# Seven half products for eight: one Strassen step in the down and output projections of a streaming encoder

## What is computed

```python
def swiglu(x, w_gate, w_up, w_down):
    return (jax.nn.silu(x @ w_gate) * (x @ w_up)) @ w_down        # 1024 -> 2816 -> 1024

for l in range(2):
    x = x + 0.5 * swiglu(rmsnorm(x, ffn1_norm[l]), ...)
    h = rmsnorm(x, mix_norm[l])
    x = x + (conv_mixer(h) if l == 0 else attn_mixer(h))          # ends in @ w_out / @ w_o, 1024 -> 1024
    x = x + 0.5 * swiglu(rmsnorm(x, ffn2_norm[l]), ...)
y = rmsnorm(x, final_norm)
```

## Time and profile before

| | |
|---|---|
| median of 3 runs | 2298.11 us (2297.57 to 2299.38) |
| span of the profiled execution, first to last instruction | 2295.8 us |
| busy: TensorE, VectorE, ScalarE, GpSimd | 99%, 43%, 28%, 4% |
| matmuls | 16584 |

### The profile page before, as it was taken

How to read it: one execution, slowest core, us unless ns; L and a number is a source line. 1 busy time by engine, 2 the same in 40 slices (tenths; PEclk the granted TensorE clock), 3 DMA queues, 4 the chain that set the end, 5 groups by cost and what they waited for, 6 DMA issues and landing times.

```text
span 2295.8 us, 39703 instructions
## 1 busy us (share of the span) xinstructions
PE 2267.1 (99%) x16584; PEld 2201.1 (96%) x16584; DVE 978.2 (43%) x1309; ACT 646.0 (28%) x967; POOL 101.6 (4%) x109
## 2 busy tenths in 40 slices
PE   7999999999999999999999999999999999999997
PEld 7999999999999999999999999987878899999997
DVE  5433333555443333345333433455455444333334
ACT  4212212422332122124221212334343432122122
POOL 1000000200100000002000000100000110000002
PEclk9999999999999999999999999999999999999999
DMA  4222222222222222223222222222222122222222
GB/s 148 83 83 83 83 83 74 86 89 83 83 77 87 80 82 82 82 72 93 83 83 83 83 83 81 85 75 73 73 72 74 57 83 80 85 78 87 76 81 69
DMA packets 55407, 187.91 MB, mean 82 GB/s; under 512 B 6864, under 2 KB 7168, under 8 KB 55312
## 3 DMA queue, kind: packets, MB, share of 16 engines
q1 hardware_dynamic: 49248, 173.76, 25.2%
q10 hardware_dynamic: 3888, 7.70, 0.9%
q0 software_dynamic: 2176, 5.09, 0.9%
HBM read 179.42 MB, written 7.09 MB: 81 GB/s over the span
## 4 chain that ended last, share of the span: by engine, by line
PE 98%; DVE 1%; DMA 1%; ACT 0%; ACTq 0%; DVEq 0%; issue 0%
PE ps L829 92%; PE ps L909 2%; PE ps L891 2%; PE ps L877 1%; DMA x<-x_t 1%; PE ps L912 0%; PE ps L844 0%; DVE sumsq L664 0%; DVE x L810 0%; PE ps L894 0%; PE ps L896 0%; DVE rstd L611 0%; PE ps L866 0%; PE ps L914 0%; ACTq L460 0%; DVE w_lo L601 0%
## 5 line engine op out<-in xcount | busy, mean ns | idle before, releaser
L829 PE MATMUL ps<-xg_hi,w_hi 128*128 128x288 f32 x3584 | 780.0, 299 | 11.1 <-DVE w_lo L601 8.6
L829 PE MATMUL ps<-xg_hi,w_lo 128*128 128x288 f32 x3584 | 768.2, 296 | 0.0
L829 PE MATMUL ps<-xg_lo,w_hi 128*128 128x288 f32 x3584 | 767.2, 296 | 0.0
L829 PEld LDWEIGHTS ps<-xg_hi,w_hi 128*128 128x128 f32 x3584 | 576.0, 189 | 42.7 <-issue 26.5
L829 PEld LDWEIGHTS ps<-xg_lo,w_hi 128*128 128x128 f32 x3584 | 577.8, 189 | 0.0
L829 PEld LDWEIGHTS ps<-xg_hi,w_lo 128*128 128x128 f32 x3584 | 577.6, 189 | 0.0
L399 ACT ACTIVATE w_hi<-w_raw 128x1024 fp32r<-128x1024 f32 (+1 forms) x336 | 346.0, 1030 | 433.6 <-PE ps L829 398.9
L601 DVE TENSOR_TENSOR w_lo<-w_raw,w_hi 128x1024 fp32r<-128x1024 f32 (+1 forms) x336 | 402.5, 1198 | 27.2 <-ACT w_hi L399 27.1
L675 DVE TENSOR_TENSOR scaled<-ps,rstd 128x576 f32<-128x576 f32 x176 | 133.3, 758 | 640.6 <-PE ps L829 640.4
L829 PE MATMUL ps<-hid_hi,w_hi 128*128 128x288 f32 x1664 | 358.2, 297 | 1.7 <-DVE hid_lo L646 1.7
L829 PE MATMUL ps<-hid_hi,w_lo 128*128 128x288 f32 x1664 | 357.2, 296 | 0.0
(11 more groups left out here) (85 smaller groups left out, 852.3 us busy)
## 6 DMA issues: line engine op xcount, KB each, us to landing
w_raw<-w SPq DMA_DIRECT2D x304, 512.0 KB, 3.6
w_raw<-w SPq DMA_DIRECT2D x32, 384.0 KB, 3.0
x<-x_t ACTq DMA_DIRECT2D x8, 288.0 KB, 10.4
k_t<-k_sb ACTq DMA_DIRECT2D x8, 288.0 KB, 2.1
v_t<-v_sb ACTq DMA_DIRECT2D x8, 288.0 KB, 2.4
bias<-bias_ext POOLq DMA_DIRECT2D x16, 128.0 KB, 3.1
bias<-bias_ext POOLq DMA_DIRECT2D x16, 112.0 KB, 2.7
y_t<-x SPq DMA_DIRECT2D x6, 288.0 KB, 2.3
```

Of the source, the lines that this page charges most:

```text
L829: mm = pe.matmul(ps[:, 2 * out_slot + b, 0:HALF], wt[:, w_slot, w], xt[:, k, b * HALF:(b + 1) * HALF], start=(k == 0 and n == 0), stop=(k ...
```

## The change

The down projections and `conv_out` are done in quads: two output tiles together, m and m+4. The weights of a quad are four blocks A11, A12, A21, A22, each half of the depth by 128 outputs, and the hidden operand is four blocks (two halves of the hidden tiles, two halves of the tokens). Seven products of sums of blocks, in Winograd's form of Strassen's step, give the four output blocks that eight products gave. Each half product is 3 x k/2 matmuls of 288 columns.

Sums of hidden blocks are made in the up phase for each pair of hidden tiles (`pair_sums`: four operations of 288 columns; `pair_hi` and `pair_lo` split the seven results in three parts: early, direct and late). Sums of weight blocks are made on VectorE, in place in a tile called the chain, between the splits: `first_sums`, then one add after the split of group 1 and one after group 2. The seven weights of a quad are split in four groups (g1 to g3 of two, g4 of one). Partial results are taken out of PSUM by ScalarE as snapshots, since a bank goes on accumulating, and VectorE makes four passes over `x` for a quad (two over snapshots, two over PSUM), where it made two.

Around this: the loops are unrolled, chunks are 8, 6 and 8 hidden tiles, `x` tiles are handled in the order 0, 4, 1, 5, ..., weight slots are three rings of two half-depth places and one place for g4, the weight blocks of a quad come in four loads of 256 KB (192 KB at depth 6), and several buffers of the attention share the memory of the new tiles, so that its first bias and cache loads start with the `qkv` phase.

```diff
-FFN_CHUNKS = (8, 8, 6)
+FFN_CHUNKS = (8, 6, 8)
...
+                if p.quads:
+                    for it in p.items:
+                        if it.u + 1 < QUADS:
+                            for b in range(3):
+                                load_direct(p.items[it.u + 1], b)
+                        if it.u + 2 < QUADS:
+                            load_chain(p.items[it.u + 2])
...
+            def load_direct(it, block_of):
+                width = it.phase.kh * P
+                if it.quad >= 1:
+                    if block_of == RAW_A22:
+                        sp.wait_ge(w_split, QUAD_ITEMS[it.quad - 1].steps["g3"].count)
+                    else:
+                        sp.wait_ge(chain_step, SUMS * (it.quad - 1) + block_of + 3)
...
+            def quads(p):
+                for it in p.items:
+                    g1, g2, g3, g4 = it.ahead
...
+                    act.wait_ge(tile_done, it.done + P1)
+                    if before:
+                        act.wait_ge(tile_read, before.evicted + 1)
+                    act.activation(snap[:, 0, :], ps[:, bank_a, 0:HALF], ACT.Copy).then_inc(snapped, 1)
+                    act.wait_ge(tile_done, it.done + P5)
+                    if before:
+                        act.wait_ge(tile_read, before.evicted + 2)
+                    act.activation(snap[:, 3, :], ps[:, bank_b, 0:HALF], ACT.Copy).then_inc(snapped, 1)
+                    split_hi(g1)
+                    act.wait_ge(tile_done, it.done + P6)
+                    act.activation(snap[:, 1, :], ps[:, bank_a, 0:HALF], ACT.Copy).then_inc(snapped, 1)
+                    split_hi(g2)
+                    split_hi(g3)
+                    if p.feeds is not None:
+                        act.wait_ge(tile_read, it.evicted + 1)
+                        if p.feeds < N_NORM - 1:
+                            xg_upper(p.feeds, first)
+                    act.wait_ge(tile_done, it.done + P7)
+                    act.activation(snap[:, 2, :], ps[:, bank_a, 0:HALF], ACT.Copy).then_inc(snapped, 1)
+                    if p.feeds is not None:
+                        squares(p.feeds, first)
+                        act.wait_ge(tile_read, it.evicted + 2)
+                        if p.feeds < N_NORM - 1:
+                            xg_upper(p.feeds, second)
+                        elif it.u == 0:
+                            act.preload_act_table(ACT.Sqrt)
+                        squares(p.feeds, second)
+                    split_hi(g4)
...
+                if w.part == "g1":
+                    first_sums(it)
+                dve.wait_ge(w_hi_done, w.count)
...
+                dve.tensor_tensor(group(w_lo, w), raw_group(w), group(w_hi, w).bitcast(F32),
+                                  ALU.subtract).then_inc(w_split, 1)
+                if w.part in ("g1", "g2"):
...
+                    dve.tensor_tensor(w_quad[:, chain, 0:width], w_quad[:, chain, 0:width], w_quad[:, direct, 0:width],
+                                      ALU.add).then_inc(chain_step, 1)
...
+                dve.tensor_tensor(w_quad[:, s3, 0:width], w_quad[:, chain, 0:width], w_quad[:, RAW_A11, 0:width],
+                                  ALU.add).then_inc(chain_step, 1)
+                dve.wait_ge(chain_step, SUMS * it.quad + 1)
+                dve.tensor_tensor(w_quad[:, chain, 0:width], w_quad[:, chain, 0:width], w_quad[:, RAW_A22, 0:width],
+                                  ALU.add).then_inc(chain_step, 1)
...
+                    split_lo(g1)
+                    split_lo(g2)
+                    dve.wait_ge(snapped, shots + 3)
+                    dve.scalar_tensor_tensor(halves(x[:, m, :]), snap[:, 0:2, :], share, halves(x[:, m, :]),
+                                             ALU.mult, ALU.add).then_inc(x_part, 1)
+                    dve.wait_ge(tile_done, it.done + P3)
+                    dve.wait_ge(x_part, 2 * it.quad + 1)
+                    dve.scalar_tensor_tensor(halves(x[:, m, :]), banks(it.slot), share, halves(x[:, m, :]),
+                                             ALU.mult, ALU.add).then_inc(tile_read, 1)
+                    split_lo(g3)
+                    dve.wait_ge(snapped, shots + 4)
+                    dve.scalar_tensor_tensor(halves(x[:, m2, :]), banks(it.slot + 1), -share, halves(x[:, m2, :]),
+                                             ALU.mult, ALU.add).then_inc(x_part, 1)
                     if p.feeds is not None and p.feeds < N_NORM - 1:
...
+                        norm_lo(p.feeds, 2 * it.u)
+                    dve.wait_ge(x_part, 2 * it.quad + 2)
+                    dve.scalar_tensor_tensor(halves(x[:, m2, :]), snap[:, 2:4, :], -share, halves(x[:, m2, :]),
+                                             ALU.mult, ALU.add).then_inc(tile_read, 1)
+                    if p.feeds is not None and p.feeds < N_NORM - 1:
+                        norm_lo(p.feeds, 2 * it.u + 1)
+                    split_lo(g4)
...
+                    pe.wait_ge(w_split, it.steps["g1"].count)
+                    half_product(it, a, s1, B11, 1, True)
+                    half_product(it, b, s1 + 1, T1, 1, True)
+                    pe.wait_ge(w_split, it.steps["g2"].count)
+                    half_product(it, c, s2, B21, 2, True)
+                    pe.wait_ge(snapped, shots + 1)
+                    half_product(it, a, s2 + 1, T2, 3, False)
+                    pe.wait_ge(w_split, it.steps["g3"].count)
+                    half_product(it, d, s3, T4, 3, True)
+                    pe.wait_ge(snapped, shots + 2)
+                    half_product(it, b, s3 + 1, B22, 2, False)
+                    pe.wait_ge(w_split, it.steps["g4"].count)
+                    pe.wait_ge(snapped, shots + 3)
+                    half_product(it, a, 6, T3, 3, False)
```

More of the change, by code:

```diff
@@ new lines, in plan @@
+        p.pairs_before = pairs - p.kh if p.quads else pairs
+        p.items = [Item(p, u) for u in range(p.n)]
+        for it in p.items:
+            it.evicted, it.ring, it.done = evicted, ring, done
+            if p.quads:
+                it.quad, it.row = quads, rows[p.k]
+                quads += 1
+                rows[p.k] += 1
+                it.slot = evicted % 4
+                it.reuses = max(in_slot.get(it.slot, -1), in_slot.get(it.slot + 1, -1))
+                in_slot[it.slot], in_slot[it.slot + 1] = evicted, evicted + 1
+                evicted += 2
+                ring += RING
+                freed += [done + P5, done + P6, done + P3]
+                done += PRODUCTS
+            else:
+                it.tile = tiles
+                tiles += 1
+                it.slot = it.u % 2 if p.kind == "qkv" else evicted % 4
+                it.reuses = in_slot.get(it.slot, -1)
+                in_slot[it.slot] = evicted
+                evicted += 1
+                ring += 1
+                done += 1
+                freed.append(done)
@@ new lines, in plan @@
+    at_ring = {w.ring: w for w in steps if w.ring is not None}
+    for n, it in enumerate(items):
+        nxt = items[n + 1] if n + 1 < len(items) else None
+        it.after = nxt
+        if it.phase.quads:
+            it.ahead = [at_ring.get(it.ring + RING + g) for g in range(RING)]
+            it.ahead.append(nxt.steps["g4"] if nxt is not None and nxt.phase.quads else None)
+        else:
+            it.ahead = [at_ring.get(it.ring + RING)]
+            if nxt is not None and nxt.phase.quads:
+                it.ahead.append(nxt.steps["g4"])
@@ L477, in up @@
+                if i == 0:
+                    split_hi(STEPS[0])
+            for w in STEPS[1:RING]:
+                split_hi(w)
+            for i in range(DT):
+                squares(0, i)
+            def up(p):
+                for it in p.items:
+                    for w in it.ahead:
+                        split_hi(w)
+                    if p.norm is not None and it.u == 0:
                         root(p.norm)
[L478 to L480 removed]
+                    if it.u % 2 == 0:
+                        act.wait_ge(tile_read, it.evicted + 1)
@@ new lines, in tiles @@
+            def tiles(p):
+                for it in p.items:
+                    if p.norm is not None and it.slot == sum_slot(p.norm) and it.u < 4:
+                        pe.wait_ge(rms_done, p.norm + 1)
+                    first = p.norm is not None and it.u == 0
+                    product(it, (xg_hi, xg_lo), PAIRED, operand_ready if first else None,
+                            DT * p.norm if first else 0)
+                    if p.norm is not None and it.u == (1 if p.norm == 0 else 0):
+                        sum_over_partitions(p.norm)
```

1006 lines of the change are left out of this document (544 added, 462 removed).

## The result

The changed kernel takes 2378.8 us (median of 4 runs, 2377.7 to 2379.4) against 2298.0 us: ratio 1.035, 95% interval 1.034 to 1.037. Forecast was 2332 us with a range of 2296 to 2362: the direction came as said, the size did not. The profiled span is 2377.3 us against 2295.8.

A forecast was written before the change was run, and what follows sets the result against it. The prediction took TensorE to bound the kernel before and VectorE's round with ScalarE the changed down stages: stages +26.6, clock +9.1, start -1.5, together +34.2 on 2298.1, so 2332 us, range 2296 to 2362.

The forecast's parts named there:

- Bound and possible gain: TensorE: a matmul stays at 0.1333 us, and 576 fewer matmuls save at most 76.8 us.
- VectorE's round: Down stages: VectorE's sums, splits and passes per quad take 12.1 us against TensorE's 11.2, at depth 6 10.2 against 8.4.
- The ring: Hand-overs between VectorE and ScalarE in each quad: 12.1 us, 10.2 at depth 6, 14.9 in stages feeding a norm.
- The first waits of a stage: TensorE waits in a down stage's first quad for the last pair's direct part: 1.2 us, 2.0 at depth 6.
- the waits for upper halves: VectorE stands through two ScalarE splits a round, about 1.1 us each, 104 waits in all.
- A22: Reload of this single-buffered 256 KB block lands in about 2.4 us, adding 0.5 us a round, 0.25 at depth 6.
- Rival D: A22 takes 3.6 us, adding 1.2 in two rounds of eight stages, +19: 2351 us; chance 0.10.
- GpSimd: An add of 1.59 us stands ahead of the sum in the final stage's longer end, +2.1 us in all.
- The clock: Slow matmuls after a stage's last wait: 1.3 us in five norm-feeding stages, half in four depth-6 ones, +9.1 (0 to 11.7).
- Rival C: Every wait over 1 us brings an unabsorbed slow stretch, some 43 x 1.3 us instead of 9.1: 2379 us; chance 0.10.
- The start: Four bias loads leave the first microseconds, so x lands earlier: -1.5 us, between 0 and 1.8.

The follow-up runs named there:

- e8: Changed kernel with block A22 in two buffers and GpSimd's adds of the squares cut to one column: 2316.8 us, ratio 1.008.
- e1: Changed kernel without its weight sums, each half product taking raw blocks: 2255.1 us, ratio 0.981 to the kernel before.
- e2: Changed kernel with block A22 in two buffers, each loaded two quads ahead: 2342.8 us, ratio 1.020 to the kernel before.
- e4: Changed kernel with 24 unread matmuls ahead of TensorE's first-snapshot wait, quads 2 to 4 of the five norm-feeding stages: 2369.3 us, ratio 1.031.
- e5: Kernel before, with only the mixer's bias and cache loads issued where the mixer's phase begins: 2291.8 us, ratio 0.9979.
- e6: Changed kernel with A22 in two buffers and, in quads 2 to 4 of a stage, all four weight sums ahead of the splits: 2278.7 us, ratio 0.992.
- e10: e6 with both xg_lo behind the last pass over x and group 4's upper half ahead of the second square: 2265.2 us, ratio 0.987.
- e11: Changed kernel with the SC block loaded behind group 4's split instead of group 3's, so A22 goes out alone: 2375.4 us, ratio 1.035.

## Why the prediction came out as it did

- **Bound and possible gain.** Right: 0.1333 us a matmul holds in half products too, and 76.8 us were to be had. The 0.130 us in four up stages, 7.7 us, stand in no row of the kernel before; they went unforeseen and are unexplained.
- **VectorE's round.** The ring was right in its links and nearly in its lengths: with the two missed causes out (e8) it is 12.35, 10.46 and 15.1 to 15.5 us where the working, without A22, gave 12.1, 10.2 and 14.9. (The terms that it lists for the first two add up to 12.2 and 10.3.) The first waits of a stage came as worked out: in e1 they cost 1.1 us in a first chunk and, where the clock stayed at 1.00, 2.0 at depth 6, for 1.2 and 2.0. So did the waits for upper halves.
- **A22, the first failing term.** The prediction took 2.4 us for 256 KB from a line through two sizes; it is 3.0 alone and 3.3 beside its neighbour. In the sum A22 had about 9 us (1.3 in each first chunk, 0.5 at depth 6, 0.3 in the others); e2 gives 36: by the table 5.0, 1.9 and, in a norm stage, 1.7. Rival D named the mechanism and a price of 19 more; the measured excess is 27, though the transfer was shorter than D's 3.6 us. D too charged the wait in two rounds of eight stages only; in after the second quad's first sums wait in every stage, 1.2 us in the norm stages where the sum had 0.3.
- **GpSimd, the second, and missing altogether.** The norm stages were summed from VectorE's and ScalarE's rows, and xg_lo's 815 ns was read as its price wherever it stands. GpSimd's row was in the same group, 1.6 us an add, and was charged only at the end of the program. With VectorE on the path, its adds cost 27 us. The 815 ns are the price of an xg_lo that starts ahead of the add; in after 12 of the 48 start behind one and take 1.8 to 2.0 us. The Trainium skill (SBUF — State Buffer, Who interferes with whom) says that a VectorE instruction with two inputs in SBUF contends with a GpSimd instruction that reads SBUF, as an exclusive lock and not as shared bandwidth. The trace agrees: 1.97 us for 0.82 behind the start of an add of 1.41, and no such lengthening of the passes that read PSUM (758 ns before, 758 and 752 in after). By that rule the term could have been foreseen: two adds a quad in 11 to 17 us.
- **The clock.** 9.1 us in the sum; its true price is not shown apart. Filling the waits of the norm stages, which had 6.5 of the 9.1, takes 9.5 us off the kernel and some 8 off these stages, so the size is right to a few us. Rival C's time, 2379, is the measured one, by chance: its mechanism is not borne out. It charges some 43 waits in full, 56 us. The mean granted clock fell from 0.997 to 0.977, which over 2377 us is 48 us if none of it had fallen into time that is waited through; e4 points to most of it having done so. In e1 waits of up to 1.3 us in a norm stage leave the granted clock at 1.00, and in e5 the very wait of the earlier trace rows does. The Trainium skill (TensorE: Matmul & The Clock Gate, HAM oscillation), by which idle gaps between groups of matmuls return the engine to half rate, agrees with the long waits of after, as the one of 5.47 us, and not with these.
- **The start.** Undersized: 1.5 us in the sum, 4.5 in after and 4.4 in e5. The bytes of the bias loads were read, not the share of the DMA engines that they held while 269 GB/s were moved.

Put together: the two failing steps are the landing of A22, taken from a line through two larger sizes, and GpSimd's adds beside VectorE, put at nothing. 2332, with A22 at 36 for 9, GpSimd at 26 for 0 (27.4, less the 1.2 us of its last add, which was in the sum), the start at -4.5 for -1.5 and -7.7 for the up stages, gives 2375; measured 2378.8. The 4 us between, and the clock's share, can't be told apart, since each experiment that shortens waits also takes slow stretches away.

## What to carry to other kernels

When an engine at 43% gets work that hands back and forth with another engine, price the round from hand to hand, not the busy time; and if it comes out over the bound, look first for operations that can be made before their partner needs them: the same adds in another order took 64 us off here (e2 to e6). An operation's duration from a trace holds for the company that it kept there, and for which of the two started first: list what runs beside it after the change, on GpSimd above all, and look at an operation's longest duration as well as its mean. A transfer of half the size is not half as long: a reload that waits for its buffer belongs into a second buffer as soon as it is in a ring.

## What was not expected of the hardware

- A GpSimd add of 1.4 us holds a VectorE operation with both inputs in SBUF that starts after it nearly until it is through (0.82 to 1.97 us, 0.69 to 1.54); one that starts 0.62 us ahead of it keeps its 0.82. Another order can hand the slowing on to the next operation (e10: the first sum at 956 ns for 683).
- 256 KB land in 3.0 us alone where 512 KB take 3.5 (medians in e11 and after): half the bytes save a seventh of the time.
- A few bias and cache loads of at most 128 KB each, issued ahead of need, held x's 2.3 MB back by 3 us at the start: 269 GB/s for 398 at the same DMA share.
- A depth-6 stage of e6 is 35.6 us or 37.1 after the same first wait of 1.76 us, the longer one with a clock of 0.95; and the wait of 1.75 us at the attention's end is followed by 0.51 in the kernel before and by 1.00 in e5. What decides between the two was not found.
- The same up stage of 576 matmuls takes 74.88 us in the changed kernels and 76.80 in the kernel before, at a granted clock of 1.00 in both. Why was not found.
